# A two-layer decoder trunk with its wide products turned round: token-major results, activations as the stationary operand

## What is computed

```python
for i in range(DEPTH):                      # DEPTH = 2
    h = rmsnorm(x, norm_g[i, 0])
    if i % 2 == 0:                          # 12 heads, q, k, v and memory queries: one product
        o_mix, q_mem = stick_breaking_mixer(h, w_in_sb[j])
    else:                                   # 12 query heads, 2 key groups, 3 branches, gates
        o_mix, q_mem = nsa_mixer(h, w_in_nsa[j], cmp_pe[j], cmp_w1[j], cmp_w2[j], cos, sin)
    o_mem = memory_attention(q_mem, rmsnorm(mem, norm_g[i, 4]), w_mem_kv[i])   # 4 heads, 256 memory tokens
    attn = jnp.concatenate([o_mix, o_mem], axis=-1) @ w_o[i]
    x = x + rmsnorm(attn, norm_g[i, 1])
    h = rmsnorm(x, norm_g[i, 2])
    x = x + rmsnorm(conv_ffn(h, w_ffn_gate[i], w_ffn_up[i], ...), norm_g[i, 3])   # D_FF = 5632
```

## Time and profile before

| | |
|---|---|
| median of 3 runs | 2437.48 us (2425.14 to 2438.07) |
| profiled execution, first to last instruction | 2423.1 us |
| TensorE busy | 2328.8 us (96%), 13346 products |
| TensorE weight loads | 2023.2 us (83%), 13346 |
| VectorE busy | 1616.9 us (67%) |
| ScalarE busy | 1325.5 us (55%) |
| GpSimd busy | 285.1 us (12%) |
| moved by DMA | 418 MB, mean 173 GB/s |

### The profile page before, as it was taken

The page is one execution under the profiler, slowest core; times in us unless marked ns, Lnnn a source line. Parts: engine busy times, 40 slices in busy tenths (PEclk is TensorE's granted clock), DMA queues, the critical chain, the costliest instruction groups (busy, mean ns, idle before and its releaser), DMA issues.

```text
span 2423.1 us, 41087 instructions
## 1 busy us (share of the span) xinstructions
PE 2328.8 (96%) x13346; PEld 2023.2 (83%) x13346; DVE 1616.9 (67%) x2422; ACT 1325.5 (55%) x1861; POOL 285.1 (12%) x316
## 2 busy tenths in 40 slices
PE   7999999979999999999979999997999999999996
PEld 6888888868888888888868888886888888888885
DVE  5666655777777777655567778767776777765555
ACT  5555554466666666544345544346666666653332
POOL 0000000210000000000034233221000000000001
PEclk9999999989999999999989999998999999999998
DMA  6544444535555555655544643353555565565553
GB/s 228 182 156 157 165 164 143 187 114 181 196 184 191 189 188 193 189 190 185 189 157 157 210 143 100 105 190 105 185 191 178 188 193 174 191 190 185 183 183 124
DMA packets 118040, 418.13 MB, mean 173 GB/s; under 512 B 13264, under 2 KB 13520, under 8 KB 117984
## 3 DMA queue, kind: packets, MB, share of 16 engines
q1 hardware_dynamic: 116784, 413.62, 52.3%
q10 hardware_dynamic: 720, 2.18, 0.3%
q0 software_dynamic: 480, 1.60, 0.2%
HBM read 414.20 MB, written 3.15 MB: 172 GB/s over the span
## 4 chain that ended last, share of the span: by engine, by line
PE 91%; DVE 5%; ACT 2%; DMA 1%; POOL 1%; issue 1%; DVEq 0%; SPq 0%; ACTq 0%; POOLq 0%
PE gemm L771 55%; PE gemm L773 28%; PE gemm L823 2%; PE SB L610 1%; PE OB L603 1%; PE SA L603 1%; DVE lo L1059 1%; PE gemm L825 1%; DVE x L1216 1%; DVE y L1210 1%; ACT hi L867 1%; PE SB L603 1%; DMA raw<-in_cmp 0%; DMA raw<-in_mem 0%; DVE rpost L1207 0%
## 5 line engine op out<-in xcount | busy, mean ns | idle before, releaser
L771 PE MATMUL gemm<-h,hi 128*128 128x512 f32 x3824 | 1351.8, 398 | 3.3 <-DVE lo L1059 2.5
L1059 DVE TENSOR_TENSOR lo<-raw,hi 128x1024 fp32r<-128x1024 f32 (+1 forms) x794 | 974.1, 1247 | 378.4 <-ACT hi L867 370.6
L773 PE MATMUL gemm<-h,lo 128*128 128x256 f32 x3824 | 1067.8, 279 | 0.0
L867 ACT ACTIVATE hi<-raw 128x1024 fp32r<-128x1024 f32 (+1 forms) x794 | 788.3, 1034 | 184.5 <-PE gemm L773 172.8
L771 PEld LDWEIGHTS gemm<-h,hi 128*128 128x128 f32 x3824 | 717.9, 188 | 175.3 <-DVE lo L1059 2.6
L773 PEld LDWEIGHTS gemm<-h,lo 128*128 128x128 f32 x3824 | 720.7, 188 | 0.6
L878 ACT ACTIVATE cross<-gemm 128x256 f32<-128x256 f32 x325 | 124.5, 383 | 749.5 <-PE gemm L773 740.0
L771 PE MATMUL gemm<-mid,hi 128*128 128x512 f32 x1408 | 494.4, 393 | 0.0
L773 PE MATMUL gemm<-mid,lo 128*128 128x256 f32 x1408 | 398.2, 283 | 0.0
L771 PEld LDWEIGHTS gemm<-mid,hi 128*128 128x128 f32 x1408 | 264.5, 188 | 61.1
L773 PEld LDWEIGHTS gemm<-mid,lo 128*128 128x128 f32 x1408 | 264.7, 188 | 0.0
(11 more groups left out here) (222 smaller groups left out, 1835.9 us busy)
## 6 DMA issues: line engine op xcount, KB each, us to landing
raw<-in_ffn SPq DMA_DIRECT2D x352, 512.0 KB, 4.2
raw<-in_in SPq DMA_DIRECT2D x138, 512.0 KB, 4.0
raw<-in_down SPq DMA_DIRECT2D x128, 448.0 KB, 4.0
raw<-in_out SPq DMA_DIRECT2D x64, 512.0 KB, 4.0
raw<-in_down SPq DMA_DIRECT2D x64, 512.0 KB, 3.9
raw<-in_mem SPq DMA_DIRECT2D x32, 512.0 KB, 4.7
raw<-in_cmp SPq DMA_DIRECT2D x16, 512.0 KB, 4.7
memT<-in_memT SPq DMA_DIRECT2D x4, 512.0 KB, 9.4
```

Of the source, the lines that this page charges most:

```text
L771: mm(out[:, 0:2 * T], hi[slot][:, at:at + P], act[:, kt, :, :].rearrange("p a t -> p (a t)"), start=k == 0, stop=False, skip_group_check=True)
L773: m = mm(out[:, T:2 * T], lo[slot][:, at:at + P], act[:, kt, 0, :], start=False, stop=k == sum(s.pieces) - 1, skip_group_check=True)
L867: act(hi[k][:, 0:kt * P], raw[k][:, 0:kt * P], ACT.Copy).then_inc(hi_done, 1)
L1059: tt(lo[k][:, 0:kt * P], raw[k][:, 0:kt * P], hi[k][:, 0:kt * P].bitcast(F32), ALU.subtract)\
```

## The change

The products turn round. The activation, 128 tokens of one k-tile, becomes the stationary operand, and the weights move, 512 wide, high and low part one after the other. A chunk is now 512 output features, and its result is token-major: 128 tokens on the partitions, in two banks, one for each half of the tokens. A piece of weights is 256 rows by 512 columns, 1024 elements on a partition as before, and asks 12 products of 512 columns. The number of pieces is 777, against 794.

- `x` and y are token-major. The sum of squares runs along the free dimension (ScalarE's accumulator, `xsq`, `ychunk`) and its factor is one number for each token; the `stats` products and GpSimd's squares go. y is multiplied by a gain row loaded with 1 MB (`gain_row`). VectorE updates chunks 0 and 2 of x, GpSimd chunks 1 and 3.
- x is brought back to feature-major by TensorE (`turnx`, 8 steps of 4 transposes for each of the four feeds), ScalarE rounds it out of PSUM, VectorE takes the rest.
- Each chunk that has to be feature-major (queries, keys, rope outputs, every gate and up chunk) is copied out with its factor by ScalarE (`evac`), transposed by TensorE (`turn`, 8 transposes) and taken on from PSUM. Values stay token-major (`keep`) and need no transpose.
- The convolution runs on ScalarE (first tap and bias) and VectorE, the gate product and the split of `mid` work in 512 columns.
- The compressor's stationary operand holds both parts side by side (60 columns), so that two products for each tile do; the gates' 36 columns get a piece of their own.
- Layer 1's memory projection moves behind down 0. The memory tokens are loaded a second time for it (`reload_mem`), into the place of `mid`; the store and reload of layer 1's keys and values goes.
- The list is one flat sequence of ticks, one for each piece; each engine handles the steps of a tick after its part of the piece, ScalarE and VectorE three pieces ahead with the weights. There are no hardware loops.

The core of the diff:

```diff
+    def stage(name, turn, dest, banks=(6, 7), rope=0, scale="h"):
+
+        k = len(s.staged)
+        s.staged.append((name, banks, dest, rope, scale))
+        do(at(name), "evac", k, on="act")
+        if rope:
+            do(at(name), "rope", k, on="dve pool")
+        do(turn, "turn", k, on="pe")
+        if dest != "ffn":
+            do(turn, "turned", k, on="dve")
...
+    def feed(f, first, before, squares):
+
+        for j in range(8):
+            t = first + (0 if j < before else j - before + 1)
+            do(t, "turnx", f, j, on="pe act dve")
+        for c in range(4):
+            do(squares + c, "xsq", f, c, on="act")
+        do(squares + 4, "rx", f, on="act dve")
+
+    def post(k, names):
+        for c, n in enumerate(names):
+            do(at(n), "ychunk", k, c, on="act dve")
+        do(at(names[3], 1), "warm", k, on="act")
+        do(at(names[3]), "post", k, on="act dve pool")
+        do(at(names[0], 5), "gain_row", k, on="sp")
...
+    for h, t in enumerate(heads):
+        do(t, "stickA", h, on="pe act dve")
+        do(t + 1, "stickB", h, on="pe act")
+        do(t + 2, "stickC", h, on="pe dve")
...
+    do(at("d03", 12), "reload_mem", on="sp")
+    for j in range(8):
+        do(at("d03", 13) + j, "feed_mem", 1, j, on="act dve")
+    do(at("mem1k", 0), "small1", on="sp")
...
+            def reload_mem():
+                sp_.wait_ge(piece_done, PLAN.at("d03", 11) + 1)
+                for q in range(4):
+                    memory(q)
+
+            def small1():
+                sp_.wait_ge(piece_done, PLAN.at("d03") + 1)
+                sp_.dma_start(pos[:], A["positions"]).then_inc(s_l1, 16)
+                sp_.dma_start(w2[:], A["cmp_w2"]).then_inc(s_l1, 16)
+                sp_.dma_start(pe[:], A["cmp_pe"]).then_inc(s_l1, 16)
+
...
+                for q in range(2):
+                    w_hi, w_lo = (w[k][:, q * W:(q + 1) * W] for w in (hi, lo))
+                    first, last = p == 0 and q == 0, p == len(c.kts) - 1 and q == 1
+                    for t in range(2):
+                        out, kt = B[c.banks[t]][:, :], kt0 + q
+                        add(out, u[:, kt, 0, half(t)], w_hi, first, False)
+                        add(out, u[:, kt, 0, half(t)], w_lo, False, False)
+                        m = add(out, u[:, kt, 1, half(t)], w_hi, False, last)
+                m.then_inc(piece_done, 1)
...
+                b = 6 + j % 2
+                take(b, h_done, 8 * f + j + 1)
+                for q in range(2):
+                    for t in range(2):
+                        kt = 2 * j + q
+                        m = tr(B[b][:, q * T + t * P:q * T + (t + 1) * P], x[:, t, kt * P:(kt + 1) * P], ident)
+                m.then_inc(xturned, 1)
...
+            def turn(k):
+                name, banks, dest, rope, _ = PLAN.staged[k]
+                if rope:
+                    pe_.wait_ge(roped_dve, ROPED.index(k) + 1)
+                    pe_.wait_ge(roped_pool, ROPED.index(k) + 1)
+                else:
+                    pe_.wait_ge(staged, 2 * k + 2)
+                for i, b in enumerate(banks):
+                    if dest == "ffn":
+                        n, up = divmod(FFN.index(k), 2)
+                        take(b, mf_done if up else conv_done, 2 * n + i + 1)
+                    else:
+                        take(b, copied, 2 * COPIED.index(k) + i + 1)
+                    for q in range(2):
+                        for t in range(2):
+                            at = (2 * i + q) * P
+                            m = tr(B[b][:, q * T + t * P:q * T + (t + 1) * P], st[:, k % 2, t, at:at + P], ident)
...
-                mm(SB[:, T:2 * T], ones, sq[:, c % 4, :], start=c == 0, stop=c == DT - 1,
-                   skip_group_check=True).then_inc(sq_read, 1)
...
-                        mm(out[:, 0:2 * T], hi[slot][:, at:at + P], act[:, kt, :, :].rearrange("p a t -> p (a t)"),
-                           start=k == 0, stop=False, skip_group_check=True)
-                        m = mm(out[:, T:2 * T], lo[slot][:, at:at + P], act[:, kt, 0, :],
-                               start=False, stop=k == sum(s.pieces) - 1, skip_group_check=True)
...
+                act_.wait_ge(piece_done, c.last + 1)
+                for t in range(2):
+                    act(st[:, k % 2, t, :], B[c.banks[t]][:, :], ACT.Copy, scale=scale_of(scale)[:, t:t + 1])\
+                        .then_inc(staged, 1)
...
+                dve.wait_ge(piece_done, c.last + 1)
+                tt(y[:, i, 1, :], B[c.banks[1]][:, :], row, ALU.mult).then_inc(y_gain, 1)
+                dve.wait_ge(y_sq, 2 * n + 1)
+                tt(y[:, i, 0, :], B[c.banks[0]][:, :], row, ALU.mult).then_inc(y_gain, 1)
...
+                nc.vector.reduce_sum(tot[:], ss[:], AX_X).then_inc(tot_done, 1)
+                dve.wait_ge(root_y, k + 1)
+                nc.vector.reciprocal(rpost[:], root[:]).then_inc(rpost_done, 1)
+                dve.wait_ge(rpost_done, k + 1)
+                for c in (0, 2):
+                    for t in range(2):
+                        at = x[:, t, c * W:(c + 1) * W]
+                        m = stt(at, y[:, c, t, :], rpost[:, t:t + 1], at, ALU.mult, ALU.add)
+                    m.then_inc(xup_dve, 1)
...
+    def wide(w):
 
         k, n = w.shape
-        return w.reshape(k // P, P, n // P, P).transpose(2, 1, 0, 3)
-
```

More of the change, by code:

```diff
@@ L89 @@
[L89 to L105, removed]
@@ L371, in tiles_in, with __init__, last @@
-def tiles_in(s, j):
-    return s.pieces[j] if j < len(s.pieces) else PIECE
-def source(s, i, j):
-    if s.pair:
-        n = j + (len(s.pieces) if s.pair == "second" else 0)
-        return s.chunk(i, n % 2 - (s.pair == "second")), sum(s.pieces[:n // 2]), s.pieces[n // 2]
-    return s.chunk(i), sum(s.pieces[:j]), s.pieces[j]
+class Chunk:
+    def __init__(self, name, w, ci, x, banks, kts=range(0, DT, 2), kind="wide", gate=None):
+        self.name, self.w, self.ci, self.x, self.banks = name, w, ci, x, banks
+        self.kts, self.kind, self.gate = list(kts), kind, gate
+        self.ticks = []
+    @property
+    def last(self):
+        return self.ticks[-1]
@@ new lines, with __init__, chunk, put @@
+class Plan:
+    def __init__(self):
+        self.pieces, self.chunks = [], {}
+        self.steps = {e: {} for e in ("pe", "act", "dve", "pool", "sp")}
+        self.staged, self.direct = [], []
+    def chunk(self, *a, **k):
+        c = Chunk(*a, **k)
+        self.chunks[c.name] = c
+        return c
+    def put(self, c, p):
+        c.ticks.append(len(self.pieces))
+        self.pieces.append((c, p))
+    def run(self, c):
+        for p in range(len(c.kts)):
+            self.put(c, p)
+    def at(self, name, p=-1, off=0):
+        return self.chunks[name].ticks[p] + off
+    def do(self, tick, step, *args, on):
+        for e in on.split():
+            self.steps[e].setdefault(tick, []).append((step, args))
@@ L384, in build @@
+PLAN = schedule()
 def build(nc, A):
@@ L390, in sem @@
             return ctx.enter_context(nc.semaphore(name))
[L393 to L401 removed]
+        views = itertools.count()
@@ new lines, in nsaC @@
+                m.then_inc(pv_ready, 1)
+            kinds = {"wide": wide, "gates": gates, "cmp": compress}
+            does = {"msum": msum, "turnx": turnx, "turn": turn, "memA": memA, "memB": memB, "memC": memC,
+                    "stickA": stickA, "stickB": stickB, "stickC": stickC, "gatesT": gatesT, "hidT": hidT, "cmp": cmp,
+                    "nsaA": nsaA, "nsaB": nsaB, "nsaC": nsaC}
+            for n, (c, p) in enumerate(PLAN.pieces):
+                pe_.wait_ge(lo_done, n + 1)
+                kinds[c.kind](c, p, n)
+                for step, args in steps("pe", n):
+                    does[step](*args)
@@ new lines @@
+    g0 = mix + 6 * kv
+    arrays["in1"] = wide(np.concatenate(
+        [parts[n] for n in ("kc", "vc", "ks", "kw", "vs", "vw")] + [nsa[:, g0 + 3 * HEADS:], nsa[:, :mix]], 1))
+    arrays["gates"] = nsa[:, g0:g0 + 3 * HEADS].reshape(DT, P, 3 * HEADS).transpose(1, 0, 2)\
+        .reshape(1, P, DT * 3 * HEADS)
+    for l in range(2):
+        arrays[f"mem{l}"] = wide(w_mem_kv[l])
+        arrays[f"out{l}"] = wide(w_o[l])
+        arrays[f"gate{l}"], arrays[f"up{l}"] = wide(w_ffn_gate[l]), wide(w_ffn_up[l])
+        arrays[f"down{l}"] = wide(w_ffn_down[l])
```

1992 lines of the change are left out of this document (855 added, 1137 removed).

## The result

The changed kernel takes 2400.79 us (median of 4 runs, 2399.93 to 2401.63) beside 2437.78 us for the kernel before (4 runs, 2425.14 to 2439.28): ratio 0.9863, 95% interval 0.9837 to 0.9889. It is faster by 1.4%, where I had put most weight on no change or slower. The profiled execution spans 2399.8 us and took 2401.63 us itself. Span against span the gain is 23.3 us, median against median 37 us; where most of that difference comes from is seen in the experiments.

What follows compares the result with a forecast made beforehand. The prediction took TensorE's queue, busy 96% of the span, as the bound. Its terms summed to +10 us on the 2423.1 us span, 2433 us; adding 14.4 us gave 2447 us, with a range of 2390 to 2497 us.

Steps and rivals of the forecast that it cites:

- wide products: TensorE's weight products: 9120 of 512 columns at 0.231 us, 2107 us in place of 2129 us: -22 us.
- statistics: TensorE's 80 products for the sums of squares removed, at 0.43 us each: -34 us.
- value transposes, compressor: Removed from TensorE: 48 value-head transposes at 0.11 us, -5 us; 64 third compressor products at 0.117 us, -7 us.
- transposes added: TensorE turns chunks needed feature-major: 600 f32 transposes at 0.11 us, +66 us.
- boundaries out to feed-forward: Two gaps from output projection to feed-forward, 15.5 us before, 10.7 us after; with slower next ticks, together -7 us.
- memory 1 and the holds: Second memory projection behind down 0: SyncE's two holds make TensorE stand 10 and 14 us; with slow restart, net +10 us.
- stickB: Attention: stickB one piece after stickA makes TensorE stand 1 us for each of 12 heads: +12 us (0 to 18).
- work at the lower clock behind gaps: TensorE's slow restart after gaps: no term of its own, only 2 us within the memory projection's holds.
- sparse heads, old waits, end: NSA heads, rope turns and window steps +5 us, layer 1's old input waits -6 us, shorter end -2 us.
- Rival B: Faster: the 512-column stream runs closer together, at 0.225 us a product, giving 2392 us; chance 0.20.
- C: Slower: the wide stream runs as in the second feed-forward, at 0.236 us a product, giving 2492 us; chance 0.20.
- The 14.4 us: Median of the old kernel's runs (2437.5 us) above its profiled span (2423.1 us), added to the forecast span.

Runs made afterwards that it cites:

- few statistics: Kernel before without 70 of its 80 products for the sums of squares: 2409.43 us, ratio 0.9916.
- turn twice: Changed kernel with every transpose of the 59 turn steps issued twice (472 more): 2449.47 us, 48.7 us above the changed kernel.
- The split experiments: 512-column products cut into two of 256: all 9120 in the changed kernel, 2508.31 us; the hi products in the kernel before, 2474.91 us.

## Why the prediction was wrong

The measured time lies inside the range, but my likeliest case was +0.4% and the kernel is 1.4% faster. The terms, spans against spans (the measured column adds to the sum by its last row, which is what is left):

| term | forecast, us | measured, us | from |
|---|---|---|---|
| wide products | -22 | -62 | 9120 x 226.7 ns = 2067 for 2129 |
| statistics | -34 | -32, an estimate | few statistics: 28 for 70 of the 80, of which 16 showed net |
| value transposes, compressor | -5, -7 | not measured alone, -12 taken over | |
| transposes added | +66 | +62 | 600 x 0.103, turn twice |
| boundaries out to feed-forward | -7 | -16 | 2 x (15.6 - 7.7) |
| memory 1 and the holds | +10 | +12 | gaps of 27.5 for 15.7 |
| stickB | +12 | +12 | 12 x (1.24 - 0.23); -13 to -15 when moved |
| work at the lower clock behind gaps | 0 (2 in the holds) | +14 | (43 - 15) / 2, an estimate from the starts |
| sparse heads, old waits, end | -3 | -1 | what is left of the sum; the end alone 20.6 to 18.8 |
| sum | +10 | -23 | spans 2423.1 and 2399.8 |

**The step that failed** is the term for the wide products, -22 us where 62 were won: the price of the wide stream, "I take 0.231 because it is what most such products take now". It measured 0.2267. That alone turned a forecast of slightly slower into faster. In the old trace a 512-column product's distance to the next start depends on its neighbour; what that trace told of both is the pair, and 346.7 ns in gate and up 0 is 226.7 + 120.0. That is one equation with two unknowns, and I split it by the starts in a place where the two kinds trade some nanoseconds (231.7 and 115.0 on average). The split experiments give the second equation: 120.0 ns for 256 columns, 226.7 ns for 512, so 13.3 ns for each product, as much as 32 columns at 2.4 GHz. Every product there has a weight load of its own, so whether the 13.3 ns belong to the product or to its load is not told apart. Of the 62 us, 40 are the 3040 products fewer at 13.3 ns (512 + 256 columns in two products before, 512 in one after). Some 22 are what the old pair cost above 346.7 ns: about 9 in gate and up 1, where the order of the widths was shown to matter, 6 in down, where a stream of one width kept the excess, and the rest in the projections. I had written "nothing is saved in columns", which is right, and then looked for a saving nowhere else, though a product costs something besides its columns. Rival B had the right mechanism in half, a part of the cost hanging on the alternation, with the place where it decides (0.2285 us) and with 2392 us near the result; I gave it 0.20 and its opposite C as much, although the mark of C (the slower second feed-forward) came from the alternation too.

"Back-to-back issue gap" in the Trainium skill's "TensorE: Matmul & The Clock Gate" gives such a fixed part as well, 2.5 ns, for a product by itself. For a stream in which each product has a weight load it gives 131 ns at 512 columns, which the prediction left out. The runs here have 226.7 ns for such a stream, 13.3 ns above its columns: the form of the first rule holds in the changed kernel, and neither figure does.

**The 14.4 us** that I added to the span belong to no kernel's surroundings. Each profiled execution took 1.8 to 2.1 us more than its span. What sets the median of before apart is seen in the one profiled execution of that length: 9 us of it are the slower pace in gate and up 0 and some 5 the clock in layer 1. That the usual execution is like it is likely, not shown. The changed kernel ran at one pace in both its profiled executions, and its four runs lie within 2 us. With 1.8 us the sum itself would have been 2435 us, and with the right price of the stream 2395 us.

**Right**: TensorE's columns set most of the pace (the wide products' loads fell by a quarter, their time by 3%); the count and price of the transposes; the reload (10 us forecast, 9.3 seen); `small1` with the squares of y behind it (14 forecast, 11.8 seen); the twelve waits of `stickB`; VectorE at 54% and ScalarE at 49% (57 and 48 forecast). **Wrong in size**: the fused updates at 1.7 us, taken from an operation beside GpSimd, took 1.05, so the boundaries won twice the forecast, before the clock; and what the lower clock behind the gaps costs, 2 us forecast and some 14 by the traces. **Not foreseen**: `angles` in ScalarE's list, 6.4 us, of the kind that I did price for `windows` but never looked for at the boundary; and rope ahead of the sparse heads' scaling, 4.3 us twice.

## What to carry to other kernels

Price a TensorE stream by two numbers, one per column and one per product, and get both from stretches of one width; where a trace shows a mixture only, an average gap of one kind is not its price in another mixture. A stretch of one width is not enough if it is one stretch only: the old layout had 226.7 ns in gate and up and 233.3 in down. Look at the spread of the runs before adding a median's excess to a span: it can be a pace that the change removes. After a turn to a written-out order, the cheap gains are steps that make a queue wait for work still ahead (a load behind a wait on SyncE, an exchange with GpSimd in ScalarE's list): here moving five of them was worth 50 us, more than the change.

## What the runs showed of the hardware

- With a weight load for each and nothing else between, a product of 256 columns takes 120.0 ns and one of 512 takes 226.7 ns: columns at 2.4 GHz and 13.3 ns. This holds with the weights moving in all stages seen, and with the weights standing still in gate and up. In down with the weights standing still it is 118.7 and 233.3 ns; the cause is open.
- In gate and up a stream alternating 512 and 256 runs at 346.7 or 353.3 ns a pair for hundreds of microseconds, in the same code of the same kernel, from one execution to the next; in the order 512, 512, 256, 256 at 348.3 ns. Its cause was not found.
- A stretch of 48 us with gaps of 12 and 6 us had a mean granted clock of 0.79; the same stage without them had 0.98. The work at the lower level behind the gaps cost 9 us beside the 25 us of the gaps themselves.
